# Near attention of a hybrid encoder: the values of a head pair formed one step later, between two heads' transposes

## The chip, the cores and the metric

The kernel runs on one core of one Trainium2 chip. The metric is the device time of one launch in microseconds (us).

## What is computed

A trunk of two layers and a final RMSNorm, applied to two groups of requests (512 positions of 1024 features each) with shared weights. Layer 0 mixes by attention, layer 1 by a chunkwise mLSTM. The change lies in layer 0, whose mixer is, cut to what matters:

```python
u = h @ w_in0
q_lat, kv_lat, k_rope, na_q, na_k, na_v, gate = split(u)
o_mla = mla(q_lat, kv_lat, k_rope, ...)           # 8 heads, every position sees all 512
o_na = neighbourhood_attn(na_q, na_k, na_v, rpb)  # 8 heads of 64, window of 8 rows x 16 columns
o = concatenate([o_mla, o_na], axis=-1) * silu(gate)
return o @ w_out0
```

For one head and one row of queries the near attention is

```python
s = einsum('bchd,bjkhd->bhcjk', q_r, k_r)
s = where(col_in, s + bias, -inf)
p = softmax(s)
o = einsum('bhcjk,bjkhd->bchd', p, v_r)
```

## The kernel before

Each engine has its own list of instructions, written out by one function per stage and engine (`c_tensor` for TensorE, `c_vector` for VectorE, `c_scalar` for ScalarE, `c_gpsimd` for GpSimd, `c_sync` for the DMA queue on SyncE). The lists are tied together by counting semaphores: `wait_ge(sem(x), at(x, n))` holds an engine until event x has occurred n times in this group of requests. An engine goes through its list in order, so whatever stands behind a waiting instruction waits too. The two groups of requests go through the stage one after the other, each in the same way.

The attention stage is one pipeline over 24 halves, numbered i. Halves 0 to 15 are the 8 far (MLA) heads, two halves each. Halves 16 to 23 are the 8 near heads, one half each, and this is where the change lies. For a near half j the work is, in order:

- scores on TensorE (`score_quad`, L1130): an even call makes both near heads of a pair at once, 24 matmuls, into PSUM banks 0 to 3. The call for half j waits for the reduction of half j - 1 (`c_max`), which reads two of these banks.
- the bias added and the maximum taken on VectorE (L1241, four custom instructions for one head, called the reduction below). It moves the scores out of PSUM into the tile `Pt[j % 4]`.
- the exponentials and their sums on ScalarE (L1287, four instructions).
- the reciprocal of the sums on VectorE (L1248).
- the scaling by it on GpSimd (L1298), counted by `c_nrm`.
- eight 128x128 transposes on TensorE (`turn`, L1149), four into PSUM bank 4 and four into bank 5. `turn(j)` waits for the scaling; its first four wait until ScalarE has copied bank 4 for half j - 1 (`c_pa`), its last four until VectorE has copied bank 5 (`c_pd`).
- these two copies: ScalarE (L1273) and VectorE (L1254), into `PT[j % 4]`.
- the values of two heads on TensorE (`values_of_two(j)` with j odd): 16 matmuls for a far pair (L1168), 24 for a near pair (`near_values`, L1187), into bank 6 or 7.
- for each c of 8 chunks of 128 output features: the product with the gate on VectorE (L1225, "gate product", counted by `d_tmp`), its rounded high part on ScalarE (L1261) and the low part on VectorE (`lo_o`, L1218, counted by `d_o`). The output projection (`out0`, lines L561 to L563) multiplies these parts.

TensorE's order is one loop over i: scores of i, transposes of i - 3, and, when i is odd, values of i - 4. VectorE's step i is: the gate product if i is in `GATED`; the low part of the product of two steps before; the reduction of half i; the reciprocal of i - 1; the copy of i - 3. ScalarE's step i: high part, copy of i - 3, exponentials of i. `out0` for the first four features stands between the last transposes and values. A "step" of the near attention below is two halves, from one call of `score_quad` to the next (i = 16, 18, 20, 22).

SyncE loads the biases of the near heads into three buffers (L1057, `T2`) and the kept gates into two (L1062, `sg0`): the bias of head 7 stands behind the gate load of chunk 5, which waits for four gate products. Then it streams the weight blocks of the coming stages (L556), one for each block whose low part VectorE has split.

Of the kernel before, what the change touches and what calls it, by code (L numbers as in the profile page):

```python
# [15 lines left out]
DC = D // P  # L16
# [67 lines left out]
def trunk(nc, xs, rows_in, fold_in, w_ada, blocks_in, up_q, up_kv, rpb_pad, const_in, out):  # L84
# [7 lines left out]
    def sem(name):  # L92
        if name not in sems:
            sems[name] = nc.alloc_semaphore(name)
        return sems[name]
# [416 lines left out]
    def group(g):  # L512

        def at(name, n):

            return PER_GROUP[name] * g + n
# [517 lines left out]
        HALVES = 2 * HEADS + HEADS  # L1034
# [8 lines left out]
        LT, LV, LO = 3, 4, 5  # L1043
        MLA_END = 2 * HEADS

        GATED = (8, 12, 16, 20, 22, 24, 26, 28)

        def s_bank(j):
            return 2 * (j % 2)
# [31 lines left out]
        def c_tensor(pe):  # L1081
            def latent_values(m):

                if m == 3:
                    pe.wait_ge(sem("b_v"), at("b_v", 1))
                elif m < 2:
                    pe.wait_ge(sem("b_act"), at("b_act", (2, 4)[m]))
                tok = slice(m * P, (m + 1) * P)
                for k in range(2):
                    last = three(pe, ps(V_BANK[m]), (lat_r[0][:, 2 + k, tok], lat_r[1][:, 2 + k, tok]),  # L1090
                                 (ukv_r[0][:, k, 512:1024], ukv_r[1][:, k, 512:1024]), k == 0, k == 1)
                last.then_inc(sem("b_vf"), 1)

            def score_pair(j):

                u, half = attention_pair(j)
                if j == 0:
                    pe.wait_ge(sem("b_qr"), at("b_qr", 4))
                    pe.wait_ge(sem("b_kpes"), at("b_kpes", HEADS - 1))
                    pe.wait_ge(sem("b_act"), at("b_act", 2 + HEADS))  # L1100
                if j == 1:
                    pe.wait_ge(sem("b_kn"), at("b_kn", 4))
                    pe.wait_ge(sem("b_kn_act"), at("b_kn_act", 2))
                if u >= 4:
                    pe.wait_ge(sem("b_qr_act"), at("b_qr_act", u - 3))
                if half == 0:
                    done = "b_kn" if u < 4 else "b_kn_act"
                    pe.wait_ge(sem(done), at(done, u % 4 // 2 * 2 + 2))
                if j >= 2:
                    pe.wait_ge(sem("c_exp"), at("c_exp", j - 1))  # L1110
                for e in range(2):
                    m = 2 * half + e
                    last = pe.matmul(ps(s_bank(j) + e), qcat[0:QK, u, m * P:(m + 1) * P], kcat[0:QK, u],  # L1113
                                     start=True, stop=True)
                last.then_inc(sem("c_s"), 1)

            def score_quad(j):

                u, half = attention_pair(j)
                n = (u - HEADS) // 2  # L1120
                if j == MLA_END:
                    pe.wait_ge(sem("c_exp"), at("c_exp", j))
                else:
                    pe.wait_ge(sem("c_max"), at("c_max", j))
                for m in range(TM):
                    for s, (a, b) in enumerate(((0, 0), (0, 1), (1, 0))):
                        for e in range(2):
                            r = 64 * e
                            o = ps(s_bank(j + e) + m // 2)[:, 2 * P * (m % 2):2 * P * (m % 2 + 1)]
                            last = pe.matmul(o.rearrange("p (b r c) -> p b r c", b=2, c=BLK_W), naq[a][r:r + 64, n, m * P:(m + 1) * P],  # L1130
                                             key_cols(nak[b][r:r + 64, n], m), start=(s == 0), stop=(s == 2))
                            if m == TM - 1 and s == 2:
                                last.then_inc(sem("c_s"), 1)
# [57 lines left out]

            for m in range(2):
                latent_values(m)
            for i in range(HALVES + LV):
                if i < MLA_END:
                    score_pair(i)
                    if i in (0, 2):
                        latent_values(2 + i // 2)
                elif i < HALVES and i % 2 == 0:
                    score_quad(i)  # L1200
                if i in (HALVES + LT - 2, HALVES + LV - 1):
                    for k in (0, 1) if i < HALVES + LT else (2, 3):
                        out0(pe, 0, k)
                if LT <= i < HALVES + LT:
                    turn(i - LT)
                if i >= LV and i % 2:
                    values_of_two(i - LV)
            for j, part in ((0, range(4, 7)), (1, range(3)), (0, (7,)), (1, range(3, DC))):
                for k in part:
                    out0(pe, j, k)  # L1210
# [4 lines left out]
        def c_vector(dve):  # L1215
            def lo_o(c):
                dve.wait_ge(sem("d_hi"), at("d_hi", c + 1))
                dve.tensor_tensor(o_D[1][:, c], otmp[c % 2], o_D[0][:, c].bitcast(F32), ALU.subtract).then_inc(sem("d_o"), 1)  # L1218

            for i in range(HALVES + 7):  # L1220
                if i in GATED:
                    c = GATED.index(i)
                    dve.wait_ge(sem("c_pv"), at("c_pv", i - LV))
                    dve.wait_ge(sem(f"sg_in{c % 2}"), at(f"sg_in{c % 2}", 16 * (c // 2 + 1)))
                    dve.tensor_tensor(otmp[c % 2], ps(6 + c % 2), sg0[:, c % 2], ALU.mult).then_inc(sem("d_tmp"), 1)  # L1225
                if i - 2 in GATED:
                    lo_o(GATED.index(i - 2))
                if i < HALVES:
                    u, half = attention_pair(i)
                    dve.wait_ge(sem("c_s"), at("c_s", i + 1))  # L1230
                    if u < HEADS:
                        dve.tensor_reduce(nmx[:, 2 * i:2 * i + 2], ps2(i % 2).rearrange("p (e t) -> p e t", e=2), AX.X,
                                          ALU.max, negate=True).then_inc(sem("c_max"), 1)
                    else:
                        h = u - HEADS
                        dve.wait_ge(sem(f"t2_in{h % 3}"), at(f"t2_in{h % 3}", 16 * (h // 3 + 1)))
                        dve.wait_ge(sem("c_t"), at("c_t", 2 * (i - 3)))
                        for m in range(TM):
                            lo, wrap = 2 * P * (m % 2), 2 * P * (m // (TM - 1))
                            n = stats(i).start + m  # L1240
                            last = dve.tensor_tensor_reduce(Pt[:, i % 4, m // 2, lo:lo + 2 * P], ps(s_bank(i) + m // 2)[:, lo:lo + 2 * P],  # L1241
                                                            T2[:, h % 3, wrap:wrap + 2 * P], -1.0, 3.0e38,
                                                            ALU.add, ALU.min, nmx[:, n:n + 1])
                        last.then_inc(sem("c_max"), 1)
                if 1 <= i < HALVES + 1:
                    j = i - 1
                    dve.wait_ge(sem("c_exp"), at("c_exp", j + 1))
                    dve.reciprocal(rinv[:, stats(j)], rsum[:, stats(j)]).then_inc(sem("c_ri"), 1)  # L1248
                if LT <= i < HALVES + LT:
                    j = i - LT  # L1250
                    dve.wait_ge(sem("c_t"), at("c_t", 2 * j + 2))
                    if j >= 4:
                        dve.wait_ge(sem("c_pv"), at("c_pv", j - 3))
                    dve.tensor_copy(PT[j % 4][:, T:2 * T], ps(5)).then_inc(sem("c_pd"), 1)  # L1254

        def c_scalar(act):
            for i in range(HALVES + LO + 1):
                if i - 1 in GATED:
                    c = GATED.index(i - 1)
                    act.wait_ge(sem("d_tmp"), at("d_tmp", c + 1))  # L1260
# [42 lines left out]
        def out0(pe, j, k):  # L1303

            b = B_OUT0 + j
            if k == 0:
                wait_split(pe, b)
                if j == 0:
                    pe.wait_ge(sem("c_max"), at("c_max", HALVES))
                if j >= 4:  # L1310
                    pe.wait_ge(sem("x_upd"), at("x_upd", j - 3))
            if j < 2:
                pe.wait_ge(sem("d_o"), at("d_o", k + 1))
            last = three(pe, ps(j % 4), (whi[:, pair_of(b), k], wlo[:, pair_of(b), k]), (o_D[0][:, k], o_D[1][:, k]),
                         k == 0, k == DC - 1)
            if k == DC - 1:
                last.then_inc(sem("blk_done"), 1)
# [954 lines left out]
```

## Time and profile before

| what | value |
|---|---|
| median of 3 runs | 1494.59 us (1493.46 to 1497.82) |
| time of the profiled execution | 1495.35 us |
| its span | 1493.2 us |
| TensorE busy | 1454.1 us (97%) |
| VectorE / ScalarE / GpSimd busy | 854.8 / 679.5 / 365.7 us |
| mean granted clock of TensorE | 0.997 of full speed |

The time of an execution is its span and about 2 us around it. Busy time counts the stretches in which an engine works on data, not those in which it waits for a semaphore. The chain of waits that ended last runs over TensorE for 84% of the span and over VectorE for 8%.

### The profile page before, as it was taken

To read this page: it belongs to the slowest core of one execution; us is meant where nothing else is said; L and a number is where in the kernel's file an instruction comes from. 1 tells how busy PE (TensorE), PEld (TensorE's weight loads), DVE (VectorE), ACT (ScalarE), POOL (GpSimd) and SP (SyncE) were. 2 spreads that over 40 slices of the span, in tenths; PEclk is the share of its full clock that TensorE was granted. 3 is DMA by queue.
4 is the path that set the end of the run, shared out by engine and by line. 5 is a ranking of instruction groups with operands and counts; after the bars stand their busy time and mean duration, and the time that the engine had idled before them with its cause. 6 is when DMAs were issued, how large, how long until landed. Compare 5 with 4: busy or idle time off the path is not lost.

```text
span 1493.2 us, 18901 instructions
## 1 busy us (share of the span) xinstructions
PE 1454.1 (97%) x7162; PEld 1111.9 (74%) x7162; DVE 854.8 (57%) x1523; ACT 679.5 (46%) x1169; POOL 365.7 (24%) x455
## 2 busy tenths in 40 slices
PE   8999999999999999999999999999999999999996
PEld 5677765678777787788888887567877778787885
DVE  7523345665787527885444344575688652788433
ACT  3323446744433435543544344674543353554233
POOL 2021023421200022765210002342120002375311
PEclk9999999999999999999999999999999999999998
DMA  9566832214332331106324533211432333111531
GB/s 385 200 220 213 254 131 86 61 59 136 106 94 83 118 108 57 43 29 240 97 89 161 141 109 117 85 57 58 155 106 85 95 111 106 50 43 45 176 93 68
DMA packets 54618, 174.27 MB, mean 117 GB/s; under 512 B 6000, under 2 KB 7408, under 8 KB 52224
## 3 DMA queue, kind: packets, MB, share of 16 engines
q1 hardware_dynamic: 54528, 173.07, 35.5%
q8 instruction: 57, 0.93, 0.3%
q14 instruction: 33, 0.27, 0.1%
HBM read 149.94 MB, written 23.10 MB: 116 GB/s over the span
## 4 chain that ended last, share of the span: by engine, by line
PE 84%; DVE 8%; ACT 4%; issue 2%; DMA 2%; POOL 1%; SPq 0%; DVEq 0%; ACTq 0%; POOLq 0%
PE ps L561 22%; PE ps L563 21%; PE ps L562 21%; PE ps L1113 3%; PE ps L1149 2%; PE ps L1168 2%; PE ps L1659 1%; PE ps L1642 1%; PE ps L303 1%; DVE w_lo L543 1%; PE ps L1693 1%; PE ps L1482 1%; PE ps L1187 1%; PE ps L1130 1%; DMA at<-z_kept 1%
## 5 line engine op out<-in xcount | busy, mean ns | idle before, releaser
L543 DVE TENSOR_TENSOR w_lo<-at,w_hi 128x1024 fp32r<-128x1024 f32 x160 | 200.0, 1250 | 347.6 <-ACT w_hi L531 347.5
L531 ACT ACTIVATE w_hi<-at 128x1024 fp32r<-128x1024 f32 x162 | 169.4, 1047 | 132.1 <-PE ps L563 124.5
L561 PE MATMUL ps<-h_e_hi,w_hi 128*128 128x512 f32 x464 | 184.3, 397 | 4.0 <-DVE w_lo L543 4.0
L563 PE MATMUL ps<-h_e_hi,w_lo 128*128 128x512 f32 x464 | 180.8, 390 | 0.0
L562 PE MATMUL ps<-h_e_lo,w_hi 128*128 128x512 f32 x464 | 180.6, 389 | 0.0
L561 PE MATMUL ps<-h_a_hi,w_hi 128*128 128x512 f32 x384 | 153.6, 400 | 2.1 <-DVE h_a_lo L593 1.3
L562 PE MATMUL ps<-h_a_lo,w_hi 128*128 128x512 f32 x384 | 149.7, 390 | 0.0
L563 PE MATMUL ps<-h_a_hi,w_lo 128*128 128x512 f32 x384 | 149.6, 389 | 0.0
L561 PEld LDWEIGHTS ps<-h_e_hi,w_hi 128*128 128x128 f32 x464 | 87.1, 188 | 38.2 <-DVE at L1468 10.1
L563 PEld LDWEIGHTS ps<-h_e_hi,w_lo 128*128 128x128 f32 x464 | 87.1, 188 | 18.6
L562 PEld LDWEIGHTS ps<-h_e_lo,w_hi 128*128 128x128 f32 x464 | 87.2, 188 | 17.7 <-issue 0.5
L561 PE MATMUL ps<-u_h_hi,w_hi 128*128 128x512 f32 x256 | 100.2, 391 | 0.0
L1298 POOL TENSOR_SCALAR at<-at,at 128x256 f32<-128x256 f32 (+1 forms) x128 | 75.6, 606 | 99.9 <-DVE at L1248 99.9
L563 PE MATMUL ps<-u_h_hi,w_lo 128*128 128x512 f32 x256 | 99.6, 389 | 0.0
L562 PE MATMUL ps<-u_h_lo,w_hi 128*128 128x512 f32 x256 | 99.6, 389 | 0.0
L1468 DVE SCALAR_TENSOR_TENSOR at<-ps,at,at 128x510 f32<-128x510 f32 (+1 forms) x128 | 95.9, 749 | 4.5
L561 PEld LDWEIGHTS ps<-h_a_hi,w_hi 128*128 128x128 f32 x384 | 72.1, 188 | 31.4 <-issue 12.0
L1570 POOL TENSOR_TENSOR at<-at,at 128x512 f32<-128x512 f32 x16 | 22.2, 1408 | 288.9 <-DMA at<-a_rows 288.9
L563 PEld LDWEIGHTS ps<-h_a_hi,w_lo 128*128 128x128 f32 x384 | 72.1, 188 | 15.3
L562 PEld LDWEIGHTS ps<-h_a_lo,w_hi 128*128 128x128 f32 x384 | 72.2, 188 | 14.5 <-issue 0.7
L573 POOL TENSOR_TENSOR at<-at,at 128x512 f32<-128x512 f32 x25 | 38.7, 1547 | 137.6 <-ACT at L1894 95.0
L1113 PE MATMUL ps<-at,at 96*128 96x512 f32 x128 | 61.4, 602 | 2.5 <-ACT at L1283 2.5
(292 smaller groups left out, 2996.5 us busy)
## 6 DMA issues: line engine op xcount, KB each, us to landing
at<-blocks_in SPq DMA_DIRECT2D x162, 512.0 KB, 3.7
at<-w_ada SPq DMA_DIRECT2D x32, 512.0 KB, 4.6
at<-w_ada SPq DMA_DIRECT2D x8, 1024.0 KB, 17.9
at<-xs SPq DMA_DIRECT2D x4, 2048.0 KB, 10.4
z_kept<-at SPq DMA_DIRECT2D x32, 256.0 KB, 2.1
at<-z_kept SPq DMA_DIRECT2D x32, 256.0 KB, 2.8
sg_kept<-at SPq DMA_DIRECT2D x16, 256.0 KB, 4.5
at<-sg_kept SPq DMA_DIRECT2D x16, 256.0 KB, 2.7
```

Source lines behind the costliest of these rows:

```text
L531: act.activation(whi[:, n % PAIRS, :, cols], wring[:, n % SLOTS, :, cols], ACT.Copy).then_inc(sem("w_hi"), 1)
L543: dve.tensor_tensor(wlo[:, n % PAIRS], wring[:, n % SLOTS], whi[:, n % PAIRS].bitcast(F32), ALU.subtract)\
L561: pe.matmul(o, stationary[0], moving[0], start=first, stop=False)
L562: pe.matmul(o, stationary[0], moving[1], start=False, stop=False)
L563: return pe.matmul(o, stationary[1], moving[0], start=False, stop=final)
L573: pool.tensor_tensor(acc, acc, sqb[:, c % 2], ALU.add).then_inc(sem("sq_added"), 1)
L1113: last = pe.matmul(ps(s_bank(j) + e), qcat[0:QK, u, m * P:(m + 1) * P], kcat[0:QK, u], start=True, stop=True)
L1149: last = pe.transpose(ps(4 + q)[:, col:col + P], Pt[:, j % 4, m, k * P:(k + 1) * P], ident)
L1168: last = pe.matmul(ps(6 + n % 2)[64 * e:64 * e + 64, 2 * P * half:2 * P * half + 2 * P], vmla[:, s, 2 * n + e], PT[(j - 1 + e) % 4][:, 2 * ...
L1298: last = pool.tensor_scalar(p, p, rinv[:, n:n + 1], 1.0, ALU.mult, ALU.mult)
L1468: dve.scalar_tensor_tensor(y[:, lo:hi], src[:, lo + d:hi + d], vb("convw", t * IC + c), y[:, lo:hi], ALU.mult, ALU.add).then_inc(sem("e_co ...
L1570: pool.tensor_tensor(chunks(Am[d], P), chunks(Abc[:, d], P), mask, ALU.subtract)\
```

## The change

The order of TensorE's list is written out for the near heads. In each near step it is now: scores of i, transposes of i - 3 (odd), values of i - 5, transposes of i - 2 (even). Before, it was: scores of i, transposes of i - 3, transposes of i - 2, values of i - 3. So the values of a pair come one step later, and stand between the two transposes. In the first near step (i = 16) there are none. Behind the last scores: transposes 21, values 19, transposes 22, `out0` for features 0 and 1, transposes 23, values 21, `out0` for 2 and 3, values 23. VectorE's gate products of chunks 3 to 6 move from the even steps 20, 22, 24, 26 to the odd steps 21, 23, 25, 27; that of chunk 7 stays at 28 and waits, in addition, for six low parts. With them move the low parts (two steps behind) and the high parts (one behind). What each gate product waits for is the same count of values as before, now in a table of its own.

```diff
-        GATED = (8, 12, 16, 20, 22, 24, 26, 28)
+        GATED = (8, 12, 16, 21, 23, 25, 27, 28)
+
+        GATED_PV = (4, 8, 12, 16, 18, 20, 22, 24)
...
-            for i in range(HALVES + LV):
-                if i < MLA_END:
-                    score_pair(i)
-                    if i in (0, 2):
-                        latent_values(2 + i // 2)
-                elif i < HALVES and i % 2 == 0:
-                    score_quad(i)
-                if i in (HALVES + LT - 2, HALVES + LV - 1):
-                    for k in (0, 1) if i < HALVES + LT else (2, 3):
-                        out0(pe, 0, k)
-                if LT <= i < HALVES + LT:
+            for i in range(MLA_END):
+                score_pair(i)
+                if i in (0, 2):
+                    latent_values(2 + i // 2)
+                if i >= LT:
                     turn(i - LT)
                 if i >= LV and i % 2:
                     values_of_two(i - LV)
+            for i in range(MLA_END, HALVES, 2):
+                score_quad(i)
+                turn(i - 3)
+                if i > MLA_END:
+                    values_of_two(i - 5)
+                turn(i - 2)
+            turn(HALVES - 3)
+            values_of_two(HALVES - 5)
+            turn(HALVES - 2)
+            for k in (0, 1):
+                out0(pe, 0, k)
+            turn(HALVES - 1)
+            values_of_two(HALVES - 3)
+            for k in (2, 3):
+                out0(pe, 0, k)
+            values_of_two(HALVES - 1)
...
                 if i in GATED:
                     c = GATED.index(i)
-                    dve.wait_ge(sem("c_pv"), at("c_pv", i - LV))
+                    dve.wait_ge(sem("c_pv"), at("c_pv", GATED_PV[c]))
+                    if c == DC - 1:
+                        dve.wait_ge(sem("d_o"), at("d_o", c - 1))
```

## Rows read from the trace of the kernel before

**Rows 1.** The profile's page, busy time of each engine.

```profile
PE 1454.1 (97%) x7162; PEld 1111.9 (74%) x7162; DVE 854.8 (57%) x1523; ACT 679.5 (46%) x1169; POOL 365.7 (24%) x455
```

**Rows 2.** Busy times by stretch: near steps 1, 3, 4, the end, the projection.

```profile
core 0: us, PE busy (x) PEld busy (x) DVE busy (x) ACT busy (x) POOL busy (x), PEclk, DMA share, GB/s
277.00:283.40 6.40, 5.83 (x58) 4.26 (x58) 5.24 (x22) 3.75 (x12) 2.13 (x4) 1.00 0.37 89
...
289.80:296.26 6.46, 5.88 (x66) 4.69 (x64) 4.97 (x21) 5.18 (x18) 3.73 (x9) 1.00 0.42 122
296.26:302.75 6.49, 5.92 (x67) 4.71 (x65) 5.72 (x22) 5.67 (x20) 3.70 (x9) 1.00 0.13 40
302.75:312.50 9.75, 9.75 (x86) 7.59 (x85) 4.79 (x8) 4.53 (x13) 2.84 (x7) 1.00 0.11 29
312.50:356.20 43.70, 43.70 (x197) 36.14 (x196) 23.52 (x27) 17.71 (x25) 11.19 (x7) 1.00 0.27 85
```

**Rows 3.** Timeline of TensorE: start, us, line, operation [idle before].

```profile
287.92 1.95 PE L1168 MATMUL ps<-at,at 128*64 128x256 f32 x16
289.80 0.39 PE L1130 MATMUL ps<-nak_hi,naq_hi 64*128 64x256 f32 x2
...
291.44 1.09 PE L1149 MATMUL ps<-at,at 128*128 128x128 f32 x8
292.88 0.63 PE L1149 MATMUL ps<-at,at 128*128 128x128 f32 x4 [0.34 <-ACT at L1273]
293.74 0.66 PE L1149 MATMUL ps<-at,at 128*128 128x128 f32 x4 [0.23 <-DVE at L1254]
294.33 2.01 PE L1187 MATMUL ps<-at,at 128*64 128x128 f32 x24
...
300.80 2.01 PE L1187 MATMUL ps<-at,at 128*64 128x128 f32 x24
...
305.20 1.06 PE L1149 MATMUL ps<-at,at 128*128 128x128 f32 x8
306.19 2.01 PE L1187 MATMUL ps<-at,at 128*64 128x128 f32 x24
...
312.49 0.50 PE L561 MATMUL ps<-o_d,w_hi 128*128 128x512 f32 x1
```

**Rows 4.** Timeline of VectorE: second reduction of step 1, then step 3.

```profile
280.79 0.41 DVE L1241 CUSTOM_DVE_ANT_0 at<-ps,at 128x256 f32<-128x256 f32 x1
...
291.55 0.42 DVE L1241 CUSTOM_DVE_ANT_0 at<-ps,at 128x256 f32<-128x256 f32 x1 [0.91 <-PE ps L1130]
...
293.02 0.66 DVE L1254 COPY at<-ps 128x512 f32<-128x512 f32 x1
293.60 0.41 DVE L1241 CUSTOM_DVE_ANT_0 at<-ps,at 128x256 f32<-128x256 f32 x1
...
296.37 0.69 DVE L1225 TENSOR_TENSOR at<-ps,at 128x512 f32<-128x512 f32 x1 [0.44 <-PE ps L1187]
296.98 0.83 DVE L1218 TENSOR_TENSOR o_d<-at,o_d 128x512 fp32r<-128x512 f32 x1
```

**Rows 5.** Timeline of ScalarE: the exponentials of half 20, and the high part.

```profile
293.05 0.51 ACT L1287 ACTIVATE at<-at,at 128x256 f32<-128x256 f32 x1 [0.32 <-DVE at L1241]
...
295.04 0.61 ACT L1261 ACTIVATE o_d<-at 128x512 fp32r<-128x512 f32 x1
```

**Rows 6.** Waits, 276 to 318 us: total us, times, longest us.

```profile
PEld ps L1149 <- issue: 2.9, 7, 0.5
```

**Rows 7.** Timeline of GpSimd: the scaling of half 19.

```profile
293.20 1.84 POOL L1298 TENSOR_SCALAR at<-at,at 128x256 f32<-128x256 f32 x4 [2.33 <-DVE at L1248]
```

**Rows 8.** DMA issues, 270 to 330 us: count, KB each, us to landing.

```profile
at<-t_masked SPq DMA_DIRECT2D x5, 256.0 KB, 2.6
```

**Rows 9.** Busy times by stretch: the near attention of the second group.

```profile
987.67:1023.10 35.43, 33.18 (x324) 25.49 (x324) 25.30 (x93) 24.79 (x80) 16.57 (x34) 1.00 0.23 68
```

**Rows 10.** Busy times by stretch: near the start, with TensorE idle in part.

```profile
20.00:30.00 10.00, 8.20 (x62) 5.00 (x62) 8.68 (x28) 3.38 (x6) 4.80 (x4) 1.00 1.01 420
```

## The prediction

> **What bounds the kernel now.** I read the page's busy shares first: TensorE is busy for 97% of the span [rows 1], so a change to the order of its work is worth what it removes of TensorE's idle time, or adds to it. Next, the busy times by stretch, one stretch for each step of the near attention [rows 2]. A step, from one group of near scores to the next, lasts 6.40 to 6.49 us of which TensorE works 5.8 to 5.9. The stretch behind the last step and the output projection behind that are full: 9.75 of 9.75 us, 43.70 of 43.70. So idle time lies in the four steps alone, and what is lost or won there moves all that follows, for nothing behind it has slack.
>
> Then the order of TensorE's instructions inside one step [rows 3]. The scores start at 289.80, eight transposes of the odd head at 291.44, and the even head's first four start only at 292.88, its last four at 293.74. Eight transposes need 0.87 us, so the first four came 0.57 us late (behind ScalarE's copy of the bank they overwrite), and the last four 0.43 us late: 293.74 is 0.72 us after VectorE began its copy at 293.02 [rows 4]. That copy sits behind the reduction of the new scores (291.55 to 293.02, with the reciprocal). With some 0.1 us more to take up the values, a step has 1.1 us of stall, and the same pattern stands four times in each group of requests. This is what the change aims at.
>
> **The change, part by part.** No instruction is added or removed except one wait; the work is reordered.
>
> *Durations used.* Scores: 1.64 us to the next TensorE instruction, 1.75 us to the reduction that waits for them [rows 3, 4]. Eight transposes: 0.87, or 0.99 when values follow (305.20 to 306.19). Far values 1.88 (287.92 to 289.80), near values 1.94; 2.04 from their start to the gate product that waits for them (294.33 to 296.37). Gate product 0.61; reduction with its reciprocal 1.47; VectorE's copy 0.58 [rows 4]. The exponentials start 1.50 us after their reduction and last 1.99 [rows 5].
>
> *One price has no row*: how soon TensorE goes on when a near reduction ends, since in this trace it never waits for one. From below, ScalarE goes on 1.50 us after the reduction's start; from above, TensorE's weight loads stood up to 0.5 us on issue at a wait [rows 6], which makes 2.0. TensorE went on 0.72 us after the start of a copy whose row lasts 0.66, thus within 0.06 us of its end, and that is nearest; I take 1.52.
>
> *Step 1* (scores 16). The two heads' transposes stay adjacent here, since the values that stood behind them move to the next step. Both stalls remain. TensorE, from 277.00 on, is through at 281.4 (1.64 + 0.87 + 0.57 + 0.43 + 0.43 + 0.44), but the next scores wait for the second reduction (it overwrites the banks): start 280.79 [rows 4] plus 1.52 is 282.31. Before, those scores began at 283.40, after 1.88 us of values; so 1.1 us is ahead on the clock while 1.88 us of work is still owed.
>
> *Step 2* (scores 18). 282.31, transposes 283.95, values 284.94, transposes 286.82, next scores 287.69. Here the design works: VectorE reduces at 284.06, copies at 285.53 and frees the bank at 286.25, before 286.82. The second reduction starts at 286.11 and ends at 287.63, just in time. The step takes 5.38 us in place of 6.40.
>
> *Step 3* (scores 20). This is the place I hold decisive. VectorE's gate product of head pair 3 now stands in the odd half-step, ahead of the second reduction, and it waits for the values that the same step makes between the two transposes. Before, it stood in the even half-step and ran under the next scores, as the one at 296.37 does [rows 4] beside scores from 296.26 on [rows 2]. Now: scores 287.69, transposes 289.33, values 290.32, gate product 292.36, reduction 292.97, and the scores of step 4 cannot start before 294.49. TensorE's own work would end at 293.07, so it stands idle for 1.4 us. The step takes 6.80 us, against 6.46 before. Queued behind the waiting gate product are the reduction, through it the exponentials and the scores, then a reciprocal that GpSimd waits for and a copy.
>
> *Step 4* (scores 22). Scores 294.49, transposes 296.13, values 297.12. The gate product waits for them until 299.16, and the low part of the product before it follows (0.6 to 0.83 us: I take 0.75, [rows 4]). The second reduction therefore starts at 300.5 where its scores had been there since 296.2. The first exponentials end at 299.7 and hold nothing; reciprocal, then VectorE's copy at 302.0. The last head's transposes (21) need that copy for their second half: 302.7. Values of 19 start at 303.3, against 300.80 before. ScalarE's copy holds their first half by the old 0.57 us, VectorE's the second half by 1.8 us.
>
> *The tail.* From 300.80 to 312.49 [rows 3], 11.69 us, TensorE ran values 19, transposes 21, and the rest. Transposes 21 are already done in the new order, so 11.69 less 0.83 to 0.87 remains: the last values end at 303.3 + 10.9 = 314.2, where they ended at 312.49. The later gate products keep their distance to their values, and the last two low parts follow the last product as now. **Sum per group: 1.7 us slower.** By stalls: 4.4 us go, and 1.1 (step 1) + 0.9 (waiting for scores 18) + 1.4 + 2.4 + about 0.3 of late take-ups come back.
>
> *The other edits.* GpSimd's scaling takes 1.84 us [rows 7] and starts right behind a reciprocal: scaling 21 starts at about 297.9 and is through at 299.8, before its transposes at 300.5; 22 and 23 are ready 1 us and more ahead. Cost nothing, unless a reciprocal comes a further 0.7 us late. The new wait of the last gate product, for the sixth low part, is met 2 us and more ahead, by an instruction earlier in its own queue (by the same walk 312.0 against 314.3): nothing. SyncE's queue: the bias of the last head stands behind a gate load that waits for gate product 3, now at 292.9 and not 290.6; with 2.6 us to land [rows 8] it is there at about 296, and its reduction comes at 300.5. The loads for the later products are issued 2 us later and needed 2 us later. The high parts on ScalarE move one half-step later, in time each time. Weight blocks are asked for by VectorE's splits in the projection, which move with it.
>
> *The second group* shows the same stretch in 35.43 us where the first has 35.50 [rows 9, 2], so it pays the same 1.7 (35.50 is 277.00 to 312.50). **Total: 3.4 us.** The profiled execution took 1495.35 us (span 1493.2); with 3.4 it comes to 1498.75. It lies 0.76 us over the median of 1494.59, so the forecast for the median is 1498.0, 0.23% slower. That is under 0.3%, about what a measurement of this kernel can tell from no change.
>
> **The rivals.**
>
> *A, slower by more than 0.3%*: TensorE's restart behind a reduction costs more than I took. The place: scores 18 and 22 in both groups, four restarts. At 0.27 us more for each, 1.1 in all, the loss passes 4.5 us; at the upper bound of 0.5 it is 5.4 us and the time 1500.0. For: weight loads did stand up to 0.5 us at waits [rows 6]. Against: after a copy TensorE lost 0.06. A gate product or low part stretched from 0.61 or 0.75 to 0.83 on the chains of steps 3 and 4 would add in the same places.
>
> *B, slightly faster*: the gate product doesn't hold the reductions (its values are in time, or TensorE has other work until then). Step 3 then takes 5.4 us and step 4 loses the 1.4 us behind gate product and low part; each group ends some 1.1 us earlier than before, and the time is 1492.5. For: VectorE has idle time in sum, 4.97 busy of 6.46 us [rows 2]. Against: the order of its queue; the values' end and the gate's start are 0.1 us apart wherever it waits.
>
> *C, faster*: all four steps shrink to 5.4 us and the held work costs nothing: 4 x 1.0 x 2 = 8.2 us, 1486.4. Against: step 1 can't, its transposes are still adjacent.
>
> *D, the clock falls.* In this stretch and where TensorE paused for 1.8 of 10 us the granted clock was 1.00 [rows 2, 10], thus 2.4 GHz; my sum leaves it there. If each of the four largest pauses (1.4 and 1.8 us) were followed by one step's 5.4 us of work at 1.2 GHz, it would take twice as long: 4 x 5.4 = 21.6 us more, about 1519.6. No row shows it. The Trainium skill (TensorE: Matmul & The Clock Gate, section on a second failure mode, psum-queue depth-cycling) says that frequent short idles between groups of matmuls can make the clock swing between its levels, which speaks against an order with longer idles; the trace's stretches with such idles do not bear it out.
>
> That the change doesn't do what it says I rule out: the order is written out in the code.
>
> **How the numbers follow.** Forecast 58%; A 24%; B 10%; C 6%; D 2%. The forecast's own range, from the bounds of low part and restart, is 1497.0 to 1499.1, with 2 or 3 in 100 spilling over 0.3%. Slower: A, D and that spill, 0.28. Faster by over 0.3%: C and a remnant, 0.07. Within: 0.65. The range from 1491.5 to 1500.5 takes in B, the forecast and most of A, with a microsecond for the median's own scatter; C and D are left out.
>
> **What would show it.** Right: steps of about 5.3, 5.4, 6.8 us; TensorE waiting for VectorE's near reduction before scores 18 and 22 (0.9 and 1.4 us); VectorE idle before gate products 3 and 4 with a reduction queued behind; the second half of transposes 21 some 1.8 us late on a copy; values ending near 314.2. Step 2 without a stall shows that the idea itself works. Wrong: step 3 at 5.4 us (B), or the restart gap behind a reduction beyond 0.3 us (A), or a granted clock below 1.00 (D).

## The result, and the profile after

The changed kernel took 1499.33 us (median of 10, 1496.54 to 1503.05) against 1494.58 us (10 runs beside it). The ratio is 1.0031, 95% interval 1.002 to 1.0043: slower by 4.7 us, where the forecast had 3.4 us. The time lies inside the stated range, but 0.2 us above the forecast's own range (1497.0 to 1499.1).

The busy times of the changed kernel by stretch: near steps 1 to 3, then scores 22 up to the start of values 19, from there to the end of the last values, and the projection. They answer to [rows 2]; columns as there.

```profile
core 0: us, PE busy (x) PEld busy (x) DVE busy (x) ACT busy (x) POOL busy (x), PEclk, DMA share, GB/s
276.10:281.41 5.31, 4.02 (x41) 3.20 (x41) 4.19 (x19) 2.66 (x10) 1.38 (x3) 1.00 0.34 98
281.41:286.99 5.58, 5.58 (x58) 4.29 (x58) 4.98 (x22) 5.58 (x21) 4.21 (x8) 1.00 0.32 98
286.99:293.77 6.78, 5.62 (x57) 4.26 (x56) 5.01 (x23) 5.51 (x20) 3.70 (x8) 1.00 0.23 52
293.77:302.46 8.69, 6.91 (x72) 5.55 (x72) 6.08 (x24) 7.01 (x24) 4.82 (x11) 1.00 0.25 84
302.46:314.75 12.29, 12.29 (x102) 9.35 (x101) 4.65 (x8) 4.16 (x10) 2.57 (x6) 0.86 0.08 23
314.75:358.45 43.70, 43.70 (x197) 36.12 (x196) 22.39 (x27) 17.68 (x25) 11.76 (x7) 1.00 0.29 85
```

Step 1 lasts 5.31 us with 1.29 us of it idle. Step 2 is full, 5.58 of 5.58 us, where a step before had 6.40: the idea works where nothing stands in its way. Step 3 lasts 6.78 us with 1.16 us of it idle, the fourth stretch has 1.78 us idle. The fifth is full by its busy time, but its granted clock is 0.86: that is new. The projection takes 43.70 us as before.

TensorE's timeline in the same execution, the rows that answer to [rows 3]:

```profile
281.41 0.39 PE L1132 MATMUL ps<-nak_hi,naq_hi 64*128 64x256 f32 x2 [0.71 <-DVE at L1255]
...
285.96 1.09 PE L1151 MATMUL ps<-at,at 128*128 128x128 f32 x8
...
293.77 0.39 PE L1132 MATMUL ps<-nak_hi,naq_hi 64*128 64x256 f32 x2 [1.17 <-DVE at L1255]
...
299.81 0.63 PE L1151 MATMUL ps<-at,at 128*128 128x128 f32 x4 [0.34 <-ACT at L1287]
301.88 0.66 PE L1151 MATMUL ps<-at,at 128*128 128x128 f32 x4 [1.43 <-DVE at L1268]
302.46 3.42 PE L1189 MATMUL ps<-at,at 128*64 128x128 f32 x24
```

The two waits for the near reduction (L1255, the old L1241) stand before scores 18 and 22. The long one before the second half of transposes 21, 1.43 us, is for VectorE's copy (L1268). And then values 19 take 3.42 us, where the same 24 matmuls took 2.01 before [rows 3]. Busy times in short stretches (columns as above) show when the clock was low: it was 1.00 during the wait, fell about a microsecond behind it, and came back between 306 and 307.

```profile
300.00:302.00 2.00, 0.57 (x5) 0.33 (x4) 1.82 (x10) 0.81 (x3) 0.66 (x2) 1.00 0.46 131
302.00:303.00 1.00, 1.00 (x12) 0.83 (x14) 0.00 (x0) 1.00 (x5) 1.00 (x3) 0.92 0.00 0
303.00:304.00 1.00, 1.00 (x10) 0.66 (x8) 0.70 (x2) 1.00 (x4) 0.61 (x2) 0.50 0.00 0
...
306.00:307.00 1.00, 1.00 (x9) 1.00 (x9) 1.00 (x2) 0.31 (x1) 0.00 (x0) 0.88 0.00 0
```

VectorE's queue shows what held both, answering to [rows 4]:

```profile
290.19 0.66 DVE L1268 COPY at<-ps 128x512 f32<-128x512 f32 x1
291.66 0.69 DVE L1239 TENSOR_TENSOR at<-ps,at 128x512 f32<-128x512 f32 x1 [0.81 <-PE ps L1170]
292.26 0.41 DVE L1255 CUSTOM_DVE_ANT_0 at<-ps,at 128x256 f32<-128x256 f32 x1
...
298.49 0.69 DVE L1239 TENSOR_TENSOR at<-ps,at 128x512 f32<-128x512 f32 x1 [0.86 <-PE ps L1189]
299.10 0.68 DVE L1230 TENSOR_TENSOR o_d<-at,o_d 128x512 fp32r<-128x512 f32 x1
299.70 0.42 DVE L1255 CUSTOM_DVE_ANT_0 at<-ps,at 128x256 f32<-128x256 f32 x1
...
301.16 0.66 DVE L1268 COPY at<-ps 128x512 f32<-128x512 f32 x1
```

Each gate product (L1239) waits 0.8 us for values that its own step makes, and the second reduction starts behind it: at 292.26, and scores 22 come 1.51 us later; at 299.70, and the copy that transposes 21 need comes at 301.16.

The measure for all that follows is **the length of the near attention** in the first group, from the start of scores 16 to the end of values 23 (the start of the next matmul). It was 35.49 us before (277.00 to 312.49), and is 38.63 here (276.12 to 314.75). Of the 3.14 us more, 1.6 are the schedule and 1.6 the clock, as the runs below separate them.

### The profile page after: what moved, and what is told of

The parts are those of the page before. It is cut to its first block, busy times and chain, and to the rows that moved or that the text cites. A ratio compares the mean times of both kernels' runs of the same rounds, so it can differ in the third digit from the quotient of the medians.

```text
span 1497.8 us, 18901 instructions
## 1 busy us (share of the span) xinstructions
PE 1455.9 (97%) x7162; PEld 1114.9 (74%) x7162; DVE 850.1 (57%) x1523; ACT 679.8 (45%) x1169; POOL 367.4 (25%) x455
## 4 chain that ended last, share of the span: by engine, by line
PE 84%; DVE 7%; ACT 4%; issue 2%; DMA 1%; POOL 1%; SPq 0%; DVEq 0%; ACTq 0%; POOLq 0%
PE ps L561 22%; PE ps L563 21%; PE ps L562 21%; PE ps L1115 3%; PE ps L1151 2%; PE ps L1170 2%; PE ps L1673 1%; PE ps L1656 1%; PE ps L303 1%; PE ps L1189 1%; PE ps L1707 1%; PE ps L1496 1%; DVE w_lo L543 1%; PE ps L1132 1%; PE ps L1726 1%
## 5 line engine op out<-in xcount | busy, mean ns | idle before, releaser
L1246 DVE TENSOR_REDUCE at<-ps 128x2 f32<-128x1024 f32 x32 | 39.2, 1224 | 42.8 <-PE ps L1115 42.8
```

## Experiments

Theory H: gate products that stand in VectorE's queue ahead of the second reductions hold TensorE. Theory C: the wait before transposes 21 lets TensorE's clock fall, and this is a cost beside it. The rivals: the new order costs by itself; moving the products costs by itself; the clock falls for another cause. A "pass" below is one group's way through the near attention, so each profile shows two.

### Both gate products one half-step later

```diff
-        GATED = (8, 12, 16, 21, 23, 25, 27, 28)
+        GATED = (8, 12, 16, 22, 24, 25, 27, 28)
...
-                    if c == DC - 1:
+                    if c >= 4:
```

The second edit lets each product from chunk 4 on wait for the low part of the chunk two before, which reads the buffer that the product overwrites. The low parts, two VectorE steps behind their products, and the high parts move with the two products.

> The new order of TensorE's list, with the gate products of chunks 3 and 4 taken out of the way of the second reductions: they move one half-step later (to the even steps 22 and 24), all else as in the changed kernel. Theory H (the gate product in VectorE's queue holds the second reduction): step 3 falls from 6.8 to about 5.4 us, TensorE's wait before scores 22 (1.2 us) is gone; the wait of transposes 21 shrinks, values 19 start 24.5 us behind scores 16 has 23.6 instead of 26.4. By the walk each group ends 2.7 us before the changed kernel and 1.1 before the old one; if the clock's drop goes too, another 1.4 us a group. Time 1492.5 us or less, ratio to before 0.998 to 0.999. Rival B2 (the new order itself is what costs, by its longer idles, wherever the gate products stand): no faster than the changed kernel, 1.003.

Measured: 1492.38 us (1491.82 to 1493.81), ratio 0.9985 (0.9977 to 0.9994); length 34.68 us. The new order of TensorE is thus no loss: with two entries of VectorE's list moved it is faster than the kernel before. The rival that the order itself costs is out. By the walk the length should have been 34.5 us; values 19 start 23.99 us behind scores 16, where 23.6 was expected. Step 3 is TensorE's own work:

```profile
289.86 1.10 PE L1151 MATMUL ps<-at,at 128*128 128x128 f32 x8
290.88 1.95 PE L1170 MATMUL ps<-at,at 128*64 128x256 f32 x16
292.76 1.09 PE L1151 MATMUL ps<-at,at 128*128 128x128 f32 x8
295.42 1.09 PE L1151 MATMUL ps<-at,at 128*128 128x128 f32 x8
...
300.24 1.17 PE L1151 MATMUL ps<-at,at 128*128 128x128 f32 x8 [0.77 <-ACT at L1287]
```

From one odd transposes to the next, 289.86 to 295.42, are 5.56 us, as in step 2. Before transposes 21 only 0.77 us is left, and it is ScalarE's copy that comes last.

### Each gate product by itself

The first kernel has 22, 23 in place of 21, 23; the second 21, 24. The wait is `c >= 4` in both.

> As the changed kernel, with the gate product of chunk 3 alone moved from step 21 to 22. Theory H: step 3 falls to 5.4 us, step 4 keeps its late second reduction; values 19 start 24.2 us behind scores 16 where the changed kernel has 26.4, so 2.1 us a group. If the clock still falls behind the wait of transposes 21, the time is about 1495; if not, 1492.5. Rival (the two holds overlap, and the second alone makes the whole delay): values 19 stay at 26 us and the time at 1499.

Measured: 1493.43 us (1492.18 to 1497.77), ratio 0.9996 (0.9986 to 1.0006); length 35.22 us.

> As the changed kernel, with the gate product of chunk 4 alone (and the low part of chunk 3, which goes behind it as before) not in front of the second reduction of step 4: 23 becomes 24. Theory H: step 3 stays at 6.8 us, transposes 21 wait 1.5 us less for VectorE's copy, values 19 start 24.8 us behind scores 16. Theory C (the clock falls because of that long wait of 1.4 us, before transposes 21): granted clock 1.00 throughout the stretch and values 19 in 2.0 us in place of 3.4. Together 2.9 us a group, time about 1493.5. Rival: the clock falls all the same, 1496.

Measured: 1494.01 us (1492.70 to 1497.63), ratio 1.0 (0.9991 to 1.0009); length 35.54 us. The waits of the two, TensorE's rows in each (scores 22 in the second alone):

```profile
299.06 0.63 PE L1151 MATMUL ps<-at,at 128*128 128x128 f32 x4 [0.77 <-ACT at L1287]
300.09 0.66 PE L1151 MATMUL ps<-at,at 128*128 128x128 f32 x4 [0.40 <-DVE at L1268]
```

```profile
292.58 0.39 PE L1132 MATMUL ps<-nak_hi,naq_hi 64*128 64x256 f32 x2 [1.17 <-DVE at L1255]
...
298.62 1.20 PE L1151 MATMUL ps<-at,at 128*128 128x128 f32 x8 [0.34 <-ACT at L1287]
```

With the first product out of the way the wait before scores 22 is gone; with the second, the 1.43 us before transposes 21. Values 19 start 24.52 and 24.85 us behind scores 16 (expected 24.2 and 24.8), against 26.34 in the changed kernel, and take 2.01 us in both groups of both kernels. Against the length of 37.06 us that the changed kernel has without the clock's fall (below), the first saves 1.84 and the second 1.52 us, both together 2.38. That is 1.0 less than the sum, and the rows show two parts of it. The first kernel moves more than its product: low part 3 goes behind too (it starts at 299.95, after the copy, and not ahead of the second reduction as at 299.10 in the changed kernel). Some 0.6 us of the second hold are gone with it: 1.22 of the 1.84 us are step 3 (6.79 to 5.57 us), the rest is this. So the two edits are not quite one hold each. The other 0.4 us are ScalarE's copy, next in line: in the kernel with both it holds transposes 21 for 0.77 us in place of 0.34.

### VectorE's part of the change with the old order of TensorE

> TensorE's list as in the kernel before, with only VectorE's part of the change (gate products at 21, 23, 25, 27, 28). Theory H: what holds is the pair of a gate product and values made in the same step; in the old order values 15 and 17 are finished before those gate products are due, so steps 3 and 4 stay at 6.46 and 6.49 us and nothing is lost there; at the end the copies behind the later products cost about 0.5 to 0.9 us a group. Time 1495.3 to 1496.3, ratio 1.0007 to 1.0012, granted clock 1.00. Rival (moving the products off the even steps costs in itself, whatever TensorE's order): steps 3 and 4 longer by 1 us and more, ratio 1.0025.

Measured: 1496.56 us (1495.26 to 1510.64), ratio 1.0022 (1.0006 to 1.0038); length 36.46 us, 0.97 more than before. Its rows of TensorE: the step before the last scores, then the end.

```profile
290.27 1.09 PE L1151 MATMUL ps<-at,at 128*128 128x128 f32 x8
...
296.73 1.09 PE L1151 MATMUL ps<-at,at 128*128 128x128 f32 x8
...
302.48 0.66 PE L1151 MATMUL ps<-at,at 128*128 128x128 f32 x4 [0.30 <-DVE at L1258]
305.02 1.06 PE L1151 MATMUL ps<-at,at 128*128 128x128 f32 x8 [0.49 <-ACT at L1277]
```

The step is 6.46 us as in [rows 2], so a product in an odd half-step costs nothing where its values are already made. Only at the end do the copies come late. The 0.97 us a group is above what I expected at most (0.9), and the ratio lies higher than expected, at 1.0007 to 1.0012, with an interval that holds it. The median is 0.5 us above what the length explains; I leave that open.

### Is it the wait that lets the clock fall?

Five idle matmuls, each of which becomes two matmuls in the trace (the expectations call these passes), between the two halves of transposes 21, written to a bank that is free:

```diff
+                    if q and j == HALVES - 3:
+                        pe.wait_ge(sem("c_max"), at("c_max", HALVES - 1))
+                        for _ in range(5):
+                            pe.matmul(ps(1)[:, 0:256], ident, Pt[:, (j - 1) % 4, 0, 0:256], start=True, stop=True)
```

> As the changed kernel, with five matmuls of 256 columns into a bank that is free put between the two halves of transposes 21, where TensorE waits 1.4 us. They compute nothing that is used. Theory C (the idle time lets the clock fall): granted clock 1.00 over the whole stretch, values 19 take 2.0 us and not 3.4, each group 1.4 us shorter, time about 1496.5, ratio 1.0012. Rival C2 (the clock falls for another cause, for instance the waits before scores 18 and 22 or a limit on the load): values 19 stay at 3.4 us and the time at 1499.

Measured: 1499.19 us (1497.08 to 1513.05), ratio 1.0044 (1.0023 to 1.0064), length 37.59 us. In this profile the clock stayed at 1.00 and values 19 took 2.01 us in both groups, but the time was not the expected 1496.5. The fill was too long: its ten matmul rows ran from 301.08 to the transposes at 303.25, 26.36 us behind scores 16, where the changed kernel has 25.76. Of these 0.6 us, 0.5 reach the length, so 1.0 us in both groups is of my own making. The rest of the miss is not explained by it: with the length of the shorter fill below, 1497.24 and 1.0 us make about 1498.2, and the median is 1499.19. Whether the clock fell in some of the executions without a profile stays open. Next, a shorter fill, three matmuls in place of five:

> As the changed kernel, with three idle matmuls (six passes, about 1.3 us) in the wait of transposes 21 where the longer fill had ten passes (2.2 us) and pushed the transposes 0.6 us back. Theory C: clock at 1.00, values 19 take 2.0 us, scores 16 to the end of values 23 in 37.2 us against 38.65 in the changed kernel and 37.58 with the longer fill; 2.9 us faster than a changed kernel in which the clock falls in both groups. Rival C2: shorter than 2 us of work is not enough to hold the clock, values 19 at 3.4 us.

Measured: 1497.24 us (1495.96 to 1498.33), ratio 1.0016 (1.0007 to 1.0024), length 37.08 us, values 19 in 2.01 us in both groups.

```profile
298.90 0.63 PE L1155 MATMUL ps<-at,at 128*128 128x128 f32 x4 [0.34 <-ACT at L1291]
299.37 1.46 PE L1148 MATMUL ps<-at,at 128*128 128x256 f32 x6
300.97 0.65 PE L1155 MATMUL ps<-at,at 128*128 128x128 f32 x4
301.55 2.01 PE L1193 MATMUL ps<-at,at 128*64 128x128 f32 x24
```

Beside it ran the changed kernel itself again.

> The changed kernel once more, unchanged, to see whether the clock's drop behind transposes 21 is in this execution as well, and with a new profile and runs beside those of the fills. If the wait decides (theory C): 3.3 to 3.4 us for values 19 in both groups, attention 38.6 us from scores 16 to the end of values 23, ratio 1.003. If chance decides: values 19 of 2.0 us in one or both groups, and attention 37.3 us there.

Measured: 1499.03 us (1496.71 to 1501.10), ratio 1.0025 (1.0016 to 1.0035). This profile shows the same wait, and no fall of the clock, in either group; length 37.07 us in the first and 37.06 in the second.

```profile
301.91 0.66 PE L1151 MATMUL ps<-at,at 128*128 128x128 f32 x4 [1.43 <-DVE at L1268]
302.50 2.01 PE L1189 MATMUL ps<-at,at 128*64 128x128 f32 x24
```

So the wait does not decide alone: of the two expected cases it was "if chance decides", with a length of 37.1 us for 37.3. A third time, with another fill:

> The changed kernel a third time, as it is, beside the fill with transposes. Theory C3 (the wait before transposes 21 lets the clock fall in some executions and not in others): median 1498.5 to 1499.5, range 4 us or more; in the profile values 19 take either 2.0 or 3.3 us in each group, with the same waits of 1.43 us ahead.

Measured: 1499.15 us (1496.19 to 1513.63), ratio 1.0039 (1.0022 to 1.0055). In the first group values 19 took 2.01 us, in the second 3.29, behind the same 1.43 us. The timeline of TensorE in the second group, then the busy times of values 19 in the two groups:

```profile
1014.61 0.98 PE L1151 MATMUL ps<-at,at 128*128 128x128 f32 x4 [1.43 <-DVE at L1268]
1015.53 3.29 PE L1189 MATMUL ps<-at,at 128*64 128x128 f32 x24
```

```profile
302.88:304.83 1.95, 1.95 (x26) 1.50 (x25) 0.77 (x2) 1.80 (x6) 1.56 (x4) 1.00 0.00 0
1015.53:1018.76 3.23, 3.23 (x26) 2.31 (x25) 0.77 (x2) 1.47 (x4) 2.24 (x5) 0.59 0.00 0
```

The granted clock was 1.00 in the one and 0.59 in the other: by the rows some four fifths of it at the lower level, 1.2 GHz, an estimate: the 1.28 us over 2.01 make 2.56 of 3.29 us at half speed.

> As the changed kernel with ten idle transposes of 128 columns (1.1 us) in place of idle matmuls in the wait of transposes 21. If they keep the clock up as the six matmul passes seem to (1497.2, range of 2.4 us): median 1497.5 and no run above 1499. If transposes don't hold the clock: median near 1499.1 and a range as wide as the changed kernel's (4.4 us), with values 19 at 3.3 us in a profile that catches it.

The edit is the fill's, with ten times `pe.transpose(ps(1)[:, 0:P], Pt[:, (j - 1) % 4, 0, 0:P], ident)`. Measured: 1496.66 us (1495.26 to 1498.79), ratio 1.0018 (1.0009 to 1.0026), length 37.04 us, values 19 in 2.01 us in both groups, waits of 0.34 us on either side of the fill. The median and the bound of 1499 came out as the first case has it; the range, 3.5 us, lies between the two.

What the profiles say together: in three profiles of the changed kernel the clock fell in 3 of 6 passes behind this wait (both groups, none, one). In the three filled ones it fell in 0 of 6, with the same waits of 0.71, 1.17 and 0.34 us ahead. In the seven others, of kernels without the 1.43 us (before, the gate products later, both and each alone, the old order, and the two of the next section), values 19 took 2.01 us in all 14. That supports theory C in its weak form: the wait makes the fall possible, and whether it comes differs from one execution to the next.

The times say less. Of the 33 runs of the changed kernel 18 took more than 1498.79 us, of the 22 with the short fill and with transposes none, at the same length of schedule; but the bound is the slowest of the 22, chosen afterwards. And of the 12 runs with the long fill five took more than 1499.8 us, the same bound with its 1.0 us added. The ratios' intervals overlap, so I call the size an estimate: the three medians of the changed kernel lie 1.8 to 2.7 us above 1497.24 and 1496.66. Single runs of 1510.64 to 1513.63 us, with a mean granted clock of 0.984 or 0.985, came in the changed kernel, with the long fill and in the old order, which has no such wait; no profile caught one, and their cause is open.

### A version that beats both

In the kernel with both products later VectorE's second reduction of step 4 began only at 298.57. On SyncE's queue the bias load of head 7 stood behind the gate load of chunk 5, which waits for gate product 3:

```profile
295.21 0.32 SPq L1064 DMA_DIRECT2D at<-sg_kept  x1
295.57 0.43 SPq L1059 DMA_DIRECT2D at<-t_masked  x1
```

Added to the gate products moved, the two loads swapped (`bias(7)` ahead of `gate(5)`):

> Both gate products later (22, 24), and on SyncE's queue the bias load of head 7 put ahead of the gate load of chunk 5. In the kernel with both gate products later alone, the second reduction of step 4 stood idle 0.9 us for that bias: its load was issued at 295.6 behind the gate load, which waits for gate product 3, and the reduction began at 298.57. Theory: with the load ahead, the reduction starts right behind the copy (297.6 on that clock), but transposes 21 wait for ScalarE's copy until 300.2 as before, so little is won: 0 to 0.3 us a group, 1492 to 1492.4. Rival: the bias was the last wait, 0.9 us a group, 1490.6.

Measured: 1492.37 us (1491.07 to 1492.91), ratio 0.9982 (0.9974 to 0.9991), length 34.60 us. The reduction now starts at 297.11, 20.24 us behind scores 16 where it was 21.22, and only 0.08 us of that reaches the end: as expected, ScalarE's copy is the last wait.

And ScalarE's copy moved ahead of its high part in each half-step:

```diff
-                if i - 1 in GATED:
-                    c = GATED.index(i - 1)
-                    act.wait_ge(sem("d_tmp"), at("d_tmp", c + 1))
-                    act.activation(o_D[0][:, c], otmp[c % 2], ACT.Copy).then_inc(sem("d_hi"), 1)
                 if i < TM:
...
                     act.activation(PT[j % 4][:, 0:T], ps(4), ACT.Copy).then_inc(sem("c_pa"), 1)
+                if i - 1 in GATED:
+                    c = GATED.index(i - 1)
+                    act.wait_ge(sem("d_tmp"), at("d_tmp", c + 1))
+                    act.activation(o_D[0][:, c], otmp[c % 2], ACT.Copy).then_inc(sem("d_hi"), 1)
```

> As the one with the bias load ahead, and ScalarE's list has the copy of bank 4 in front of the high part in each half-step, not behind it. Theory: transposes 21 wait only for exponentials 22 and the copy, 0.5 us less, so each group ends 0.5 us earlier than there; time about 1491.3, ratio 0.998. Rival: the high parts come late and hold the low parts and the projection, no gain.

Measured: 1492.15 us (1490.92 to 1495.79), ratio 0.9982 (0.9972 to 0.9992), length 34.20 us. The wait before transposes 21 fell from 0.78 to 0.34 us and the length by 0.40, near the 0.5 expected; the two medians are 0.2 us apart, too little to tell them apart by time, and the expected 1491.3 us was not reached.

## Why the prediction was right, point by point

- **The schedule** came out as walked. Taking 0.9 us off each clock time (scores 16 start at 276.12, not 277.00): step 1 ends at 281.41 for 281.41; gate product 3 at 291.66 for 291.46; scores 22 at 293.77 for 293.59; the second reduction of step 4 at 299.70 for 299.6; transposes 21 are held until 301.88 for 301.8; values 19 start at 302.46 for 302.4. The schedule costs 1.57 us a group (37.06 less 35.49) where I had 1.7. The idle times of the rows, 0.71, 1.17 and 1.43 us, are 0.2 to 0.4 us below the 0.9, 1.4 and 1.8 forecast; before, too, a late start that the walk counted as 0.57 or 0.43 us stands in the rows as 0.34 or 0.23. That the sum fits so well is in part luck: step 2 was 0.2 us longer, the low part 0.15 us shorter, and the end from values 19 on took 10.69 us where I had 10.9.
- **The restart behind a reduction**, the price without a row: 1.51 us in place of the assumed 1.52 (279.90 to 281.41, 292.26 to 293.77). Rival A had no part in the loss, though the measured 4.7 us is the size that it priced (4.5); only the rows tell it from the clock.
- **Step 2** took 5.58 us for 5.38. From transposes 16 to the next scores TensorE needed 1.03 us (285.96 to 286.99) where I had 0.87: 0.16 us that I counted as take-up between transposes and values only.
- **Low part**: in VectorE's queue it took 0.60 us (299.10 to 299.70) where I took 0.75, between 0.6 and 0.83; its row lasts 0.68.
- **Rivals B and C** fell with the holds: the products do wait for the values of their own step. The experiment with both products later gives the size of B, 0.8 us a group where I had 1.1.
- **The clock** is where the sum was short, and a granted clock below 1.00 was one of my own signs of being wrong. The step that failed is the term that I put at nothing: "the granted clock was 1.00 [rows 2, 10], thus 2.4 GHz; my sum leaves it there". I had argued from the idle shares of two stretches of the old kernel; its near attention has single waits of at most 0.34 us, and the stretch from 20 to 30 us none above 0.79. Rival D named the mechanism, but gave it 2%, all four pauses and a whole step of 5.4 us for each. The traces show it behind one pause a group, in about half of the passes, for 1.6 us each time: in the first of them values 19 longer by 1.41 and the stretch behind by 0.2. With 3 of 6 passes that is about 1.6 us in the mean of an execution, an estimate, and 3.1 at most.
- **The Trainium skill** (TensorE: Matmul & The Clock Gate, section on psum-queue depth-cycling) says that short idles between groups of matmuls can make the clock swing. I wrote that the trace does not bear it out. The trace of the changed kernel does in part, with a granted clock of 0.86 over 302.46 to 314.75: it shows one fall, behind the longest of its waits, and not a swing with each short idle. For the waits of 0.23 and 0.34 us of the near attention before, no row here shows it.
- Schedule 3.1 us and clock about 1.6 us make 4.7, as measured. The first is read from the rows; the second rests on six passes, and the near agreement should not be taken for a proof of it.

## What to carry to other kernels

When work on one engine is moved to fill a stall, ask of every queue that reads its result where the reader now stands, and what is queued behind it. Here a 0.6 us product that waited for the moved values held the reduction on which the next scores wait, and two numbers in a list, with the wait that goes with them, decided between 0.3% slower and 0.15% faster. A walk through the queues with durations from the trace placed each event to 0.2 us; what it could not see was the clock.

## What the runs showed of the hardware that was not expected

- The same program with the same waits ran values 19 at a granted clock of 1.00 in one pass and 0.59 in another. It fell in 3 of 6 passes behind a wait of 1.43 us that followed waits of 1.17 and 0.34 us, and in none of the six passes seen when idle matmuls or transposes, of 1.25 to 2.32 us by their rows, stood in that wait.
- The clock also falls in a place that the change doesn't touch. In all 13 profiles TensorE waits 0.98 or 0.99 us at about 40 us; over 40 to 60 us the granted clock was then 0.91 to 0.94 in ten of them, and 1.00 in three: the kernel before, the third profile of the changed kernel, the short fill. So a comparison of single executions mixes in a second such chance. What it costs there isn't shown: from the matmul behind that wait to the one at about 54 us it was 14.49 us with the fall (changed kernel) and 14.45 without (before).
- Transposes served as fill in the two passes seen: clock 1.00 in both groups, median 1496.66 us beside 1497.24 with the matmuls. The same page of the Trainium skill, in its section on the PE-mode transpose, says that transposes don't count as busy in the same way. These runs show no difference, though with a fall in only half of the passes without a fill, and waits of 0.34 us on either side of this one, they can't show that transposes alone keep the clock up.
- Idle work has its own price: the fill that overran its wait made each group 0.5 us longer, and its median, 1499.19 us, was no better than that of the kernel without a fill.
